# Two-part products in the gates of the position terms, and one wide product for both token parts in the first MLP product

## The reference

```python
        hn = rms(h, g_mlp_pre[i])
        y = jnp.square(jax.nn.relu(hn @ w_mlp_in[i])) @ w_mlp_out[i]
        h = h + rms(y, g_mlp_post[i])
        gate = jax.nn.sigmoid(h @ w_ple_gate[i])
        h = h + gate * (p[i] @ w_ple_proj[i])
```

## Time and profile before

| | |
|---|---|
| median of 3 runs | 2334.57 us (2332.36 to 2337.82) |
| time of the profiled execution | 2337.61 us |
| its span, first to last instruction | 2335.8 us |
| TensorE matmul busy | 1918.1 us (82%) |
| TensorE weight load busy | 1202.8 us (51%) |
| VectorE busy | 835.9 us (36%) |
| ScalarE busy | 702.7 us (30%) |
| GpSimd busy | 182.8 us (8%) |
| chain that ended last, by engine | PE 54%, DMA 36%, DVE 5%, ACT 3% |

### The profile page before, as it was taken

How to read it: one execution, slowest core, us unless ns; L and a number is a source line. 1 busy time by engine, 2 the same in 40 slices (tenths; PEclk the granted TensorE clock), 3 DMA queues, 4 the chain that set the end, 5 groups by cost and what they waited for, 6 DMA issues and landing times.

```text
span 2335.8 us, 27342 instructions
## 1 busy us (share of the span) xinstructions
PE 1918.1 (82%) x11120; PEld 1202.8 (51%) x11120; DVE 835.9 (36%) x1517; ACT 702.7 (30%) x1238; POOL 182.8 (8%) x187
## 2 busy tenths in 40 slices
PE   6999999999986656565556755668989999989998
PEld 5766787789941111111111111117749985758985
DVE  4353877865640000000000000006646543546643
ACT  4243567665320000000000000004445432355531
POOL 1100122261020000000000000001000000110000
PEclk9999999999988778878888788878889999999999
DMA  8543234445789999999999999993405554404552
GB/s 352 207 144 141 101 118 127 130 125 196 276 361 429 428 427 429 428 429 428 428 429 428 428 428 428 428 427 133 174 20 188 181 180 183 163 19 172 181 198 108
DMA packets 66003, 619.03 MB, mean 265 GB/s; under 512 B 8032, under 2 KB 16736, under 8 KB 21360
## 3 DMA queue, kind: packets, MB, share of 16 engines
q1 hardware_dynamic: 54304, 598.98, 63.7%
q10 hardware_dynamic: 9248, 10.49, 1.9%
q0 software_dynamic: 2352, 8.19, 1.0%
HBM read 616.52 MB, written 1.11 MB: 264 GB/s over the span
## 4 chain that ended last, share of the span: by engine, by line
PE 54%; DMA 36%; DVE 5%; ACT 3%; issue 1%; POOL 0%; SPq 0%; DVEq 0%; ACTq 0%; POOLq 0%
DMA ring<-in_w_edown 17%; DMA ring<-in_w_eup 17%; PE bank L502 11%; PE bank L503 11%; PE bank L504 11%; PE bank L2579 2%; PE bank L590 2%; PE bank L2845 2%; PE bank L2604 2%; PE bank L561 2%; PE bank L1199 1%; PE bank L1775 1%; PE bank L1107 1%; PE bank L575 1%; DMA ring<-in_w_ada 1%
## 5 line engine op out<-in xcount | busy, mean ns | idle before, releaser
L473 DVE TENSOR_TENSOR ring_parts<-ring,ring_parts 128x2048 fp32r<-128x2048 f32 (+1 forms) x110 | 247.7, 2256 | 172.2 <-ACT ring_parts L467 167.6
L467 ACT CAST ring_parts<-ring 128x2048 fp32r<-128x2048 f32 (+1 forms) x136 | 251.2, 1848 | 175.8 <-DMA ring<-in_w_mlp_out 89.0
L2652 DVE TENSOR_TENSOR work<-bank,work 128x512 f32<-128x512 f32 x14 | 9.7, 692 | 802.5 <-PE bank L2579 802.5
L2579 PE MATMUL bank<-ring,work 128*32 128x512 f32 x1024 | 166.1, 782 | 134.9 <-DMA ring<-in_w_egate 70.2
L2604 PE MATMUL bank<-ring,work 128*32 128x512 f32 x1024 | 176.4, 827 | 102.1 <-DMA ring<-in_w_edown 95.2
L484 POOL TENSOR_TENSOR ring_parts<-ring,ring_parts 128x512 fp32r<-128x512 f32 x92 | 120.6, 1343 | 1216.6 <-ACT ring_parts L467 1216.6
L2579 PE MATMUL bank<-work 128*32 128x512 f32 x1024 | 149.5, 716 | 72.2 <-DMA work<-in_w_eup 62.5
L502 PE MATMUL bank<-hT_hi,ring_parts 128*128 128x256 f32 (+2 forms) x584 | 196.7, 337 | 0.3 <-issue 0.3
L504 PE MATMUL bank<-hT_hi,ring_parts 128*128 128x256 f32 (+2 forms) x584 | 187.4, 321 | 0.0
L502 PE MATMUL bank<-hn_hi,ring_parts 128*128 128x256 f32 x640 | 184.3, 288 | 3.8 <-DVE hn_lo L693 3.8
L503 PE MATMUL bank<-hT_lo,ring_parts 128*128 128x256 f32 (+2 forms) x584 | 187.3, 321 | 0.0
(11 more groups left out here) (386 smaller groups left out, 3118.4 us busy)
## 6 DMA issues: line engine op xcount, KB each, us to landing
ring<-in_w_edown SPq DMA_DIRECT2D x64, 2048.0 KB, 26.3
work<-in_w_eup SPq DMA_DIRECT2D x33, 2048.0 KB, 25.9
ring<-in_w_egate SPq DMA_DIRECT2D x33, 2048.0 KB, 25.9
work<-in_w_egate SPq DMA_DIRECT2D x31, 2048.0 KB, 25.9
ring<-in_w_eup SPq DMA_DIRECT2D x31, 2048.0 KB, 26.2
ring<-in_w_mlp_in SPq DMA_DIRECT2D x32, 1024.0 KB, 4.8
ring<-in_w_mlp_out SPq DMA_DIRECT2D x32, 1024.0 KB, 4.8
ring<-in_w_ada SPq DMA_DIRECT2D x12, 2048.0 KB, 9.8
```

What stands on the lines that cost most here:

```text
L467: act.copy(halves_of(name, ring_parts)[1], halves_of(name, ring)[0]).then_inc(hi_made, 1)
L473: dve.tensor_tensor(lo, halves_of(name, ring)[0], hi, ALU.subtract).then_inc(lo_made, 1)
L2579: last = pe.matmul(bank[which][32 * n:32 * n + 32, :], rows[:, 2 * c + k2, :], w[:, k2, 512 * n:512 * n + 512], start=c == 0 and k2 == 0, ...
```

## The change

The gates use `product3`. For that their weights come as four chunks of 1 MB (half h, k group u) and are split like the others: the upper parts by ScalarE between and after the two halves of the post norm, the lower parts of chunks (0,0), (0,1), (1,1) by VectorE and of (1,0) by GpSimd. GpSimd holds back its last piece until the lower parts before it are made. The transposed residual is stored as hi and lo parts (`hn_hi`, `ple_lo`).

In the first MLP product, hi weights times both token parts is one matmul of 512 columns into a whole bank (columns 0 to 255 the hi tokens, 256 to 511 the lo ones), followed by lo weights times hi tokens with 256 columns. The two halves are then added: ScalarE copies columns 256 to 511 to SBUF, VectorE adds the other half, which frees the bank, and a third VectorE operation makes relu and square in one; rounding and lower part now read SBUF.

```diff
--- before.py
+++ after.py
@@ -173,7 +173,7 @@
-    for n, kt, width in (("mlp_in", KT, 256), ("mlp_out", 4, 512), ("ple_proj", 2, D), ("ple_gate", KT, 512)):
+    for n, kt, width in (("mlp_in", KT, 256), ("mlp_out", 4, 512), ("ple_proj", 2, D), ("ple_gate", 4, 512)):
@@ -426,9 +426,10 @@
...
                       None if last < 1 else (rows_ready, ROWS[f"dn{l}"] + 3 + h), True)
-            for i in range(2):
-                chunk(f"pg{l}{i}", d["w_ple_gate"][l, 0, i], KT, 512,
-                      (gemm_ready, GROUP[f"ple{l}"] + 3 + i))
+            for h in range(2):
+                for u in range(2):
+                    chunk(f"pg{l}{h}{u}", d["w_ple_gate"][l, u, h], 4, 512,
+                          (gemm_ready, GROUP[f"ple{l}"] + 3 + h) if u else None, True)
@@ -474,13 +475,15 @@
...
-        def split_lower_pool(pool, name):
+        def split_lower_pool(pool, name, beside=False):
...
             for c in range(0, kt * n, PIECE):
+                if beside and c + PIECE >= kt * n:
+                    pool.wait_ge(lo_made, SPLIT.index(name))
                 ins = pool.tensor_tensor(lo[:, c:c + PIECE], whole[:, c:c + PIECE], hi[:, c:c + PIECE], ALU.subtract)
@@ -610,10 +613,10 @@
...
         hn = work[:, 0:KT * L].rearrange("p (k l) -> p k l", k=KT)
-        hn_hi = parts_in_work("hn_hi", [P, KT, L], 0)
         xnm = work[:, KT * L:KT * L + TT * D].rearrange("p (t n) -> p t n", t=TT)
         AFTER_N = KT * L + TT * D
-        hn_lo = parts_in_work("hn_lo", [P, KT, L], AFTER_N)
+        hn_parts = parts_in_work("hn_parts", [P, 2, AFTER_N // L, L], 0)
+        hn_hi, hn_lo = (hn_parts[:, i, 0:KT, :] for i in range(2))
@@ -680,7 +683,9 @@
...
                 if mul is None:
-                    dve.tensor_copy(dst, src).then_inc(hn_made, 1)
+                    hi, lo = (x[:, 4 * j:4 * j + 4, t * P:(t + 1) * P] for x in (hn_hi, ple_lo))
+                    link(dve.tensor_copy(hi, src))
+                    dve.tensor_tensor(lo, src, hi, ALU.subtract).then_inc(hn_made, 1)
                     continue
@@ -2685,13 +2690,16 @@
...
         tab_in, pT_in = sem("tab_in"), sem("pT_in")
-        hid_relu, hid_squared, hid_rounded = sem("hid_relu"), sem("hid_squared"), sem("hid_rounded")
+        hid_crossed, hid_squared, hid_rounded, hid_made = sem("hid_crossed"), sem("hid_squared"), sem("hid_rounded"), sem("hid_made")
...
         rm = Region(HID + 2 * DFF // P * L)
-        hid_r = rm.take(2, L)
+        HID_BUFS = 4
+        hid_s = rm.take(HID_BUFS, L)
+        ple_lo = parts_in_work("ple_lo", [P, KT, L], rm.at)
+        assert rm.at + KT * L <= WORK - 2 * L - TT * D - 512
         tmpm = xnm.rearrange("p t (h n) -> p (t h) n", h=2)
@@ -2727,7 +2735,6 @@
...
         def mlp_pe(pe, l):
-            rows = hn_hi, hn_lo
             for i in range(UPS):
@@ -2738,8 +2745,10 @@
...
                             wait_turned(pe, (ATTENTION, LATENT)[l], 3 + k // 4)
-                        last = product3(pe, bank[n % 4][:, 0:L], [x[:, k, b * P:(b + 1) * P] for x in w], [x[:, k, :] for x in rows],
-                                        k == 0, k == KT - 1)
+                        hi, lo = (x[:, k, b * P:(b + 1) * P] for x in w)
+                        pe.matmul(bank[n % 4][:, :].rearrange("p (i l) -> p i l", i=2), hi, hn_parts[:, :, k, :],
+                                  start=k == 0, stop=False, skip_group_check=True)
+                        last = pe.matmul(bank[n % 4][:, 0:L], lo, hn_hi[:, k, :], start=False, stop=k == KT - 1, skip_group_check=True)
                     last.then_inc(gemm_ready, 1)
@@ -2750,12 +2759,12 @@
...
             for i in range(DOWNS - 2):
-                pe.wait_ge(gemm_freed, GROUP[f"up{l}"] + 4 * i + 4)
+                pe.wait_ge(hid_made, 2 * UPS * l + 4 * i + 4)
                 for h in range(2):
...
                     last.then_inc(chunk_used, 1)
-            pe.wait_ge(gemm_freed, GROUP[f"up{l}"] + 2 * UPS)
+            pe.wait_ge(hid_made, 2 * UPS * (l + 1))
@@ -2776,24 +2785,29 @@
...
             def round_hid(m):
-                n = GROUP[f"up{l}"] + m
-                act.wait_ge(hid_squared, 32 * l + m + 1)
-                act.copy(hid_hi[:, m, :], bank[n % 4][:, 0:L]).then_inc(hid_rounded, 1)
+                act.wait_ge(hid_squared, 2 * UPS * l + m + 1)
+                act.copy(hid_hi[:, m, :], hid_s[:, m % HID_BUFS, :]).then_inc(hid_rounded, 1)
...
                     act.wait_ge(gemm_ready, n + 1)
-                    if m >= 2:
-                        act.wait_ge(hid_squared, 32 * l + m - 1)
-                    act.activation(hid_r[:, m % 2, :], bank[n % 4][:, 0:L], ACT.Relu).then_inc(hid_relu, 1)
+                    if m >= HID_BUFS:
+                        act.wait_ge(hid_made, 2 * UPS * l + m - HID_BUFS + 1)
+                    act.copy(hid_s[:, m % HID_BUFS, :], bank[n % 4][:, L:2 * L]).then_inc(hid_crossed, 1)
                     if m >= 1:
...
                 split_upper(act, u)
-            close_act(act, MLP + 3 * l, rows_ready, [ROWS[f"dn{l}"] + j + 1 for j in range(4)], tmpm)
+            counts_of = [ROWS[f"dn{l}"] + j + 1 for j in range(4)]
+            post_act(act, MLP + 3 * l, rows_ready, counts_of, tmpm, 0)
+            split_upper(act, f"pg{l}00")
+            split_upper(act, f"pg{l}01")
+            post_act(act, MLP + 3 * l, rows_ready, counts_of, tmpm, 1)
+            split_upper(act, f"pg{l}10")
+            split_upper(act, f"pg{l}11")
@@ -2801,23 +2815,37 @@
...
             def lower_hid(m):
-                n = GROUP[f"up{l}"] + m
-                dve.wait_ge(hid_rounded, 32 * l + m + 1)
-                dve.tensor_tensor(hid_lo[:, m, :], bank[n % 4][:, 0:L], hid_hi[:, m, :], ALU.subtract).then_inc(gemm_freed, 1)
+                dve.wait_ge(hid_rounded, 2 * UPS * l + m + 1)
+                dve.tensor_tensor(hid_lo[:, m, :], hid_s[:, m % HID_BUFS, :], hid_hi[:, m, :], ALU.subtract).then_inc(hid_made, 1)
...
                 for m in (2 * i, 2 * i + 1):
-                    b = bank[(GROUP[f"up{l}"] + m) % 4][:, 0:L]
-                    dve.wait_ge(hid_relu, 32 * l + m + 1)
-                    dve.tensor_tensor(b, b, hid_r[:, m % 2, :], ALU.mult).then_inc(hid_squared, 1)
+                    n = GROUP[f"up{l}"] + m
+                    s = hid_s[:, m % HID_BUFS, :]
+                    dve.wait_ge(hid_crossed, 2 * UPS * l + m + 1)
+                    dve.tensor_tensor(s, s, bank[n % 4][:, 0:L], ALU.add).then_inc(gemm_freed, 1)
                     if m >= 1:
                         lower_hid(m - 1)
+                    dve.wait_ge(gemm_freed, n + 1)
+                    dve.scalar_tensor_tensor(s, s, 0.0, s, ALU.max, ALU.mult).then_inc(hid_squared, 1)
                 split_lower(dve, units[i + SPLIT_EARLY + 1])
...
             dve.wait_ge(grow_loaded, 16 * (2 * l + 2))
-            close_dve(dve, MLP + 3 * l, tmpm)
+            end = MLP + 3 * l
+            for h in range(2):
+                gained(dve, end, tmpm, 0, h)
+            residual(dve, end, tmpm, 0)
+            gained(dve, end, tmpm, 1, 0)
+            turned_tile(dve, end, 0)
+            split_lower(dve, f"pg{l}00")
+            split_lower(dve, f"pg{l}01")
+            gained(dve, end, tmpm, 1, 1)
+            residual(dve, end, tmpm, 1)
+            dve.wait_ge(lo_made, SPLIT.index(f"pg{l}11"))
+            split_lower(dve, f"pg{l}11")
+            turned_tile(dve, end, 1)
@@ -2836,13 +2864,16 @@
...
-                    wait_chunk(pe, f"pg{l}{h}")
-                    wg = slot(f"pg{l}{h}")
                     pe.wait_ge(gemm_freed, n - 3)
                     for k in range(KT):
-                        if h == 0 and k % 4 == 0:
-                            wait_turned(pe, end, (2, 2, 3, 4)[2 * t + k // 4])
-                        last = pe.matmul(bank[n % 4][:, :], hn[:, k, t * P:(t + 1) * P], wg[:, k, :], start=k == 0, stop=k == KT - 1)
+                        if k % 4 == 0:
+                            wg = split_chunk(pe, f"pg{l}{h}{k // 4}")
+                            if h == 0:
+                                wait_turned(pe, end, (2, 2, 3, 4)[2 * t + k // 4])
+                        last = product3(pe, bank[n % 4][:, :], [x[:, k, t * P:(t + 1) * P] for x in (hn_hi, ple_lo)],
+                                        [x[:, k % 4, :] for x in wg], k == 0, k == KT - 1)
+                        if t == 1 and k == 3:
+                            last.then_inc(chunk_used, 1)
                     last.then_inc(gemm_ready, 1)
@@ -2858,21 +2889,19 @@
...
         def ple_dve(dve, l):
+            link = stepper(dve, dve_step)
             for t in range(TT):
...
                     dve.wait_ge(pp_taken, 4 * l + 4)
-                    dve.tensor_tensor(gterm[:, h, :], ppl[:, t, 512 * h:512 * h + 512], gs[:, t, 512 * h:512 * h + 512], ALU.mult).then_inc(gate_put, 1)
-                    dve.wait_ge(gate_put, 4 * l + 2 * t + h + 1)
```

(4 more changed lines are left out.)

## The result

The changed kernel took 2340.47 us (median of 12 runs, 2336.28 to 2346.21), the kernel before on the same chips 2333.65 us (12 runs). The ratio is 1.0026, 95% interval 1.0017 to 1.0036: slightly slower, by some 6 us (the two medians differ by 6.8). The forecast was 2336.1 us, within a range of 2330 to 2343. The time is inside that range, but above the line of 2339.3 us from which the prediction spoke of "slower" (chance 0.25), and above its main case's own range of 2331 to 2339; the forecast had +1.5 us and the runs +6.

A forecast was written before the change was run, and what follows sets the result against it. TensorE was taken to bound the kernel. Terms of -6.7 (first MLP product), +3.4 and +1.6 (gates, layers 0 and 1) and +3.2 us (clock) gave +1.5 on 2334.6, so 2336.1 us, range 2330 to 2343.

The forecast's parts named there:

- main case: Whole kernel: gates start late and the clock drops, +1.5 us, 2336.1 us, own range 2331 to 2339; chance 0.60.
- Rival 3: First MLP product: the ScalarE and VectorE loop becomes the bound; at 6.3 us a turn 2343.2 us; chance 0.12.
- Rival 4: First MLP product: the wide matmul pays for two runs (0.240 us), no 6.7 us saved, 2342.8 us; chance 0.08.
- The first MLP product: Both layers: a pair of matmuls takes 0.347 us where three took 0.360, saving 6.7 us in all.
- The loop of ScalarE and VectorE: First MLP product: one turn takes 5.55 us, level with TensorE's unit, and costs nothing under about 6.0 us.
- The start of the gates: Ahead of layer 0's gates: TensorE stalls 6.95 us, VectorE's subtraction standing behind tile 1's square and ScalarE's two casts.
- The clock: Start of each layer's gates: after idling, TensorE runs at the lower clock, losing 1.6 us a layer.
- Rival 1: Start of the gates: the clock stays up despite the idle time, 2332.9 us; chance 0.14.
- The second tile: Gates, tile 1: restart takes 2.0 us in place of 1.3; in layer 0 a further 1.6 us stall for the norm.
- Rival 2: Gates: they are not late, the sum is -17.3 us, 2317.3 us; chance 0.06.

The follow-up runs named there:

- the kernel without GpSimd: The changed kernel with the subtraction of gate chunk (1,0) on VectorE, behind `gained` of tile 1, instead of GpSimd; 2338.47 us, ratio to before 1.0022.
- the new order: The changed kernel, VectorE doing transposed tile 0 and subtractions (0,0), (0,1) before tile 1's work, and (1,0) instead of GpSimd; 2323.16 us, ratio to before 0.9958.
- the pair that separates it: The kernel without GpSimd, and the same with 52 unused transposes on TensorE ahead of the gates; 2338.47 and 2335.53 us, ratios 1.0022 and 1.0013.

## Why the prediction was right, and where it was off

The range held and the chain of waits was the forecast one, step by step; the size was 6 us and not 1.5. That the range held is in part luck: it reached above 2339 us only for rivals 3 and 4, and neither came about as described. The main case was short by some 6 us in the profile: 3.3 us in the first MLP product and 1.4 us in each layer's gates.

**The first MLP product** was mis-sized. The step to 0.227 + 0.120 = 0.347 us a pair, 6.7 us saved, measured 0.354 us, 3.3 us saved, in the profile of the changed kernel. It was worked out from a row with matmuls of one width only, and the bounds given (0.227 to 0.240) held what was found. The prediction named a step of the wide matmul other than 0.227 as a sign of being wrong, and this sign came: it is 0.233 to 0.241 here. The 0.347 us do occur, in 7 of 18 stages, with steps of 0.230 to 0.233 and a narrow matmul shorter than 0.120, so the term is one of two values. Rival 4, with 0.240 because of the two runs, had half of the loss and not its cause. The rule of the Trainium skill ("TensorE: Matmul & The Clock Gate", the section on 56 ns and 53.3 ns), weighed there, would give 2.5 ns a pair by an estimate from that page; the runs show 6.5 or 13 ns.

**The loop of ScalarE and VectorE** was right: 5.58 us measured, 5.55 forecast, and no wait of TensorE. Rival 3 is out.

**The start of the gates** was right in its cause. In size it was exact in layer 0, from start to start: the last matmul before the stall began at 1933.20 and takes 0.23, the first of the gates began at 1940.38, 6.95 us of lost time and 6.95 forecast. Against the kernel without GpSimd, the new order moves nothing but instructions of VectorE, and it took the stall away. But layer 1 had 7.8 us, and so had seven of the eight stages profiled with this order and GpSimd beside it (7.71 to 7.89 us behind the second MLP product; layer 0 of the changed kernel alone has 6.79). The missing term is that VectorE and GpSimd take turns: the prediction let both subtract at once, each at its price of being alone (2.29 us, and 1.26 us a piece), although it had placed them on top of each other in time. Where GpSimd is first, VectorE's (0,0) waits for one piece, 1.1 us. The exact hit in layer 0 hangs on a start 0.04 us ahead of GpSimd's, and is luck. So is that GpSimd's chunk (1,0) cost nothing there: it was made some 4 us later than forecast, half a microsecond before TensorE, slowed by its clock, came to it.

**The clock** was right in kind, and too small in layer 0. Against the forecast of 1.6 us a layer (bounds 0 and 1.85) the pair that separates it shows 2.1 and 1.6 us. In the changed kernel 12 matmuls of layer 0 and 6 of layer 1 stepped at 0.427 us in place of 0.227, and the first step of 0.56 us was 0.26 above that of a restart at full clock: by these rows an estimate of 2.7 and 1.5 us. Rival 1 is out.

**The second tile** was right: restart after 2.2 us (forecast 2.0), in layer 0 a wait for the norm of 1.6 us from start to start (forecast 1.6; the profile calls 1.4 of them idle), none in layer 1. The gates' excess over their forecast, 1.4 us in either layer, is then: in layer 0 the clock (1.1) and 0.2 at the restart; in layer 1 GpSimd's turn (1.0) and 0.2 at the restart. The rest, 0.1 to 0.3 us, is the slower first steps behind each restart and, in layer 1, that the sum took the end before from a modelled end (13.97 us), 0.16 us later than one counted from start to start.

**Rival 2**, gates in time, was priced at -17.3 us. The new order comes near its condition and shows -10 us: a pause of 1 us at chunk (1,0) in each layer, the norm's wait in layer 0 and the slower pace of the wide product are the rest.

## What to carry to other kernels

Work that replaces a slow product with a faster one pays only if what it needs is made in time, and that is decided by the order in which each engine's program is written: before adding a preparation, write down which instruction it stands behind and which stands behind it, on every engine. An idle time on TensorE as long as these (6.7 to 7.9 us) costs its length and then a stretch at the lower clock. Subtractions on VectorE and GpSimd that fall together should be priced one behind the other, not each alone; ScalarE's casts beside them kept their 1.9 us.

## What the runs showed of the hardware

- A pair of `fp32r` matmuls, 512 and 256 columns, repeated without a pause, runs at 0.347 or at 0.354 us a pair; the pace is kept for a whole stage of 90 us, and two stages of one execution can differ. Reading one run of 512 columns or two of 256 does not explain it: one run gave the slower pace in both its stages, two runs gave either. What chooses is not known. Three matmuls of 256 columns showed one pace only, 0.360 us.
- VectorE's and GpSimd's subtractions take turns: the one that starts first keeps its time, the next takes about 3.3 us, be it 128 x 2048 float32 on VectorE (2.29 us alone) or a piece of 128 x 512 on GpSimd (1.26 us). GpSimd's four pieces took 9.5 to 10.0 us, 5.03 us in the earlier trace rows. Two of VectorE's operations on 512 columns (L738) took 2.67 us in place of 1.42.
- After 6.7 to 7.9 us without work TensorE's granted clock was 0.50, 1.2 GHz, at its next matmul, in every kernel here that had such an idle time, and 6 to 13 matmuls passed at that pace. With 52 small transposes in that time it stayed at 1.00, although 1.0 to 2.0 us of idle time were left ahead of the gates.
